# Streaming encoder trunk on one core: the first up quad's weight sums moved from VectorE to adding DMAs, two token differences moved from GpSimd to VectorE

## The reference, cut to what matters

```python
n = rms_norm(x, ln1_w); proj = n @ w_in            # 1024 x 3584, split into q k v g, gate_b gate_c hc
x = x + concatenate([retention(q,k,v,g), gate_b * conv3(gate_c * hc)]) @ w_out      # 1024 x 1024
h2 = rms_norm(x, ln2_w)
x = x + square(relu(h2 @ w_up)) @ w_down           # 1024 x 4096 and 4096 x 1024
```

## Time and profile before

| | us |
|---|---|
| median of 3 runs | 1407.86 (1407.82 to 1409.0) |
| the profiled execution's own time | 1408.8 |
| its span | 1407.1 |
| PE busy | 1377.2 (98% of the span) |
| DVE busy | 947.0 (67%) |
| ACT busy | 618.1 (44%) |
| POOL busy | 191.4 (14%) |

### The profile page before, as it was taken

The page is one execution under the profiler, slowest core; times in us unless marked ns, Lnnn a source line. Parts: engine busy times, 40 slices in busy tenths (PEclk is TensorE's granted clock), DMA queues, the critical chain, the costliest instruction groups (busy, mean ns, idle before and its releaser), DMA issues.

```text
span 1407.1 us, 21462 instructions
## 1 busy us (share of the span) xinstructions
PE 1377.2 (98%) x7702; PEld 1236.7 (88%) x7702; DVE 947.0 (67%) x1144; ACT 618.1 (44%) x736; POOL 191.4 (14%) x193
## 2 busy tenths in 40 slices
PE   8999999998999999999999999999899999999997
PEld 6888999888889899899878889998798998998986
DVE  5336415988975966867861473278889678688586
ACT  5311221466636446446543012134574464464463
POOL 2343200021000000000032430000400000000001
PEclk9999999999999999999999999999999999999999
DMA  7424203525454645555142242054166455544623
GB/s 273 135 76 121 83 1 128 134 84 122 110 159 121 145 100 142 146 118 158 31 138 96 90 121 68 3 158 140 46 150 150 103 142 145 120 120 120 150 60 105
DMA packets 93728, 162.39 MB, mean 115 GB/s; under 512 B 3956, under 2 KB 21492, under 8 KB 93624
## 3 DMA queue, kind: packets, MB, share of 16 engines
q1 hardware_dynamic: 74472, 123.18, 26.0%
q0 software_dynamic: 19008, 37.75, 15.8%
q10 hardware_dynamic: 144, 0.07, 0.0%
HBM read 153.58 MB, written 7.41 MB: 114 GB/s over the span
## 4 chain that ended last, share of the span: by engine, by line
PE 94%; DVE 2%; issue 2%; ACT 1%; POOL 1%; DMA 0%; DVEq 0%; SPq 0%; POOLq 0%; ACTq 0%
PE pair L808 27%; PE pair L867 25%; PE pair L653 15%; PE pair L663 12%; PE pair L880 8%; PE pair L703 2%; PE pair L741 1%; PE pair L748 1%; PE pair L722 1%; DVE ring L1755 1%; DVE x L1801 1%; PE pair L726 1%; PE pair L731 1%; DMA w_raw<-in_w_in 0%; PE pair L734 0%
## 5 line engine op out<-in xcount | busy, mean ns | idle before, releaser
L808 PE MATMUL pair<-mlp_in_hi,ring 128*128 128x320 f32 x1792 | 400.1, 311 | 9.8 <-DVE hidden L1780 9.8
L1141 ACT ACTIVATE ring<-raws 128x1024 fp32r<-128x1024 f32 x248 | 259.8, 1057 | 290.1 <-PE pair L867 150.2
L867 PE MATMUL pair<-ring,a_ring 128*128 128x512 f32 x1632 | 380.4, 390 | 0.0
L1755 DVE TENSOR_TENSOR ring<-raws,ring 128x1024 fp32r<-128x1024 f32 x248 | 305.2, 1241 | 101.6 <-ACT ring L1141 100.1
L867 PEld LDWEIGHTS pair<-ring,a_ring 128*128 128x128 f32 x1632 | 305.5, 188 | 63.6
L808 PEld LDWEIGHTS pair<-mlp_in_hi,ring 128*128 128x128 f32 x1792 | 302.7, 189 | 11.2 <-DVE ring L1755 10.3
L808 PE MATMUL pair<-mlp_in_lo,ring 128*128 128x320 f32 x896 | 278.2, 310 | 0.0
L808 PEld LDWEIGHTS pair<-mlp_in_lo,ring 128*128 128x128 f32 x896 | 169.6, 189 | 0.2
L663 PE MATMUL pair<-norm_hi,ring 128*128 128x320 f32 x512 | 114.5, 310 | 0.0
L1801 DVE TENSOR_TENSOR x<-x,pair 128x512 f32<-128x512 f32 x160 | 103.3, 678 | 11.4 <-PE pair L867 11.4
L653 PE MATMUL pair<-ring,norm_hi 128*128 128x512 f32 x320 | 101.6, 399 | 3.2 <-DVE norm_lo L1563 3.1
(11 more groups left out here) (153 smaller groups left out, 1686.2 us busy)
## 6 DMA issues: line engine op xcount, KB each, us to landing
raws<-in_w_mlp_up SPq DMA_DIRECT2D x32, 1024.0 KB, 5.3
raws<-in_w_mlp_down SPq DMA_DIRECT2D x32, 1024.0 KB, 5.0
w_raw<-in_w_in SPq DMA_DIRECT2D x27, 1024.0 KB, 6.1
raws<-in_w_mlp_up POOLq DMA_DIRECT2D x16, 1024.0 KB, 9.1
raws<-in_w_mlp_down POOLq DMA_DIRECT2D x16, 1024.0 KB, 8.8
raws<-in_w_out SPq DMA_DIRECT2D x8, 1024.0 KB, 8.4
past_state<-in_state_ret SPq DMA_DIRECT2D x8, 512.0 KB, 4.5
out_ret_s<-past_state SPq DMA_DIRECT2D x8, 512.0 KB, 4.9
```

The source lines that it names most:

```text
L808: mm = pe.matmul(out[:, n, 0:HALF], item_half(item, h, a)[:, k, n * P:(n + 1) * P], mlp_in[i][c][:, k], start=(i in (B11, B21, SUM_1112, B ...
L867: mm = pe.matmul(out[:], a_item[:, a, 2 * h + k, pair * P:(pair + 1) * P], item_half(item, h, c)[:, k], start=(i in (B11, B21, SUM_1112) a ...
L1141: nc.scalar.activation(item_half(item, h, 0), raw_half(quad, RAW_OF[i], h), ACT.Copy).then_inc(half_hi.sem, 1)
L1755: nc.vector.tensor_tensor(item_half(item, h, 1), raw_half(quad, RAW_OF[i], h), f(item_half(item, h, 0)), ALU.subtract).then_inc(half_lo.se ...
```

## The change

For quad 1 (the first up quad) alone, in each layer, the sums of SUM_1112 and SUM_111222 are made by DMAs of POOL's queue that add half quarters (0.5 MB) from HBM onto the slot of "11", instead of by four VectorE instructions. They signal `first_summed[h]`. The add of "22" onto "12" of quad 1 now waits only for the quarter "12" to be there, since no instruction reads the raw "12" for a sum any more. s2 and s3 are made by VectorE instead of GpSimd. The order on ACT and DVE in `up(0)` is written anew.

```diff
+BY_DMA = 1
...
 def sums_to(quad, product, half):
-    return quad * len(SUMS) + SUMS.index((product, half)) + 1
+    assert quad != BY_DMA
+    skipped = len(SUMS) if quad > BY_DMA else 0
+    return quad * len(SUMS) + SUMS.index((product, half)) + 1 - skipped
...
-        weights_summed = Signal("weights_summed", QUADS * len(SUMS))
+        weights_summed = Signal("weights_summed", (QUADS - 1) * len(SUMS))
+        first_summed = [Signal(f"first_summed{h}", 32) for h in range(2)]
...
@@ ACT, weight_half
+                    elif quad == BY_DMA:
+                        act.wait_ge(first_summed[h].sem, first_summed[h].at(layer, 16 if i == SUM_1112 else 32))
@@ ACT, up(0)
                         weight_half(item + 1, 1)
+                        weight_half(item + 2, 0)
                         read_tile(4)
                         in_diff_hi_of(0)
-                        weight_half(item + 2, 0)
+                        weight_half(item + 2, 1)
                         copy_product(b, B11, 1)
+                        weight_half(item + 3, 0)
                         in_diff_hi_of(1)
-                        weight_half(item + 2, 1)
-                        weight_half(item + 3, 0)
+                        copy_product(b, SUM_1112, 0)
+                        weight_half(item + 3, 1)
+                        copy_product(b, SUM_1112, 1)
                         in_diff_hi_of(2)
-                        copy_product(b, SUM_1112, 0)
-                        copy_product(b, SUM_1112, 1)
-                        weight_half(item + 3, 1)
                         weight_half(item + 4, 0)
+                        weight_half(item + 4, 1)
                         copy_product(b, SUM_111222, 0)
-                        weight_half(item + 4, 1)
@@ POOL
+                def add_half(i, h):
+                    quad, (last, name) = BY_DMA, {SUM_1112: (B11, "12"), SUM_111222: (SUM_1112, "22")}[i]
+                    pool.wait_ge(half_lo.sem, half_lo.at(layer, 2 * (quad * PRODUCTS + last) + h + 1))
+                    settle(pool)
+                    pool.dma_start(raw_half(quad, "11", h), quad_weights(layer, quad, name)[:, :, h * 256:(h + 1) * 256],
+                                   accum_op=ALU.add).then_inc(first_summed[h].sem, 16)
                 for quad in range(QUADS):
-                    pool.wait_ge(weights_summed.sem, weights_summed.at(layer, sums_to(quad, SUM_1112, 1)))
+                    if quad == BY_DMA:
+                        slot = slot_of(quad, "12")
+                        pool.wait_ge(slot_in[slot].sem, slot_in[slot].at(layer, 16 * (quad + 1)))
+                    else:
+                        pool.wait_ge(weights_summed.sem, weights_summed.at(layer, sums_to(quad, SUM_1112, 1)))
                     add_onto(quad, "12", "22", onto_12)
+                    if quad == BY_DMA:
+                        for h in range(2):
+                            add_half(SUM_111222, h)
                     pool.wait_ge(half_lo.sem, half_lo.at(layer, 2 * (quad * PRODUCTS + SUM_111222) + 2))
                     add_onto(quad, "11", "21", onto_11)
                     if quad == 0:
-                        for t in range(NT):
+                        for t in range(3):
                             row_rstd(layer, NT, t)
-                        last = TURN["n2", NT - 1, 1]
-                        pool.wait_ge(turn_lo.sem, turn_lo.at(layer, split_turns_to(last)))
-                        nc.gpsimd.tensor_tensor(s2_raw[:], t_diff[:], t11[:], ALU.subtract).then_inc(s2_ready.sem, 1)
-                        nc.gpsimd.tensor_tensor(t21[:], t11[:], t21[:], ALU.subtract).then_inc(s3_ready.sem, 1)
+                        add_half(SUM_1112, 0)
+                        for t in range(3, NT):
+                            row_rstd(layer, NT, t)
+                        add_half(SUM_1112, 1)
@@ DVE, up(0); next_difference makes s2, third_difference waits for s2 and makes s3
                         weight_half(item, 1)
                         normalise(layer, NT, 3, ORDER[3], 32)
+                        weight_half(item + 1, 0)
                         normalise(layer, NT, 4, ORDER[4], 32)
-                        weight_half(item + 1, 0)
                         read_turn_lo(layer, ("n2", 3, 1))
                         weight_half(item + 1, 1)
                         read_turn_lo(layer, ("n2", 4, 1))
-                        weight_sum(q, SUM_1112, 0)
+                        weight_half(item + 2, 0)
                         in_diff_lo_of(0)
-                        weight_half(item + 2, 0)
                         hidden_sum(b, B21, 0)
-                        weight_sum(q, SUM_1112, 1)
+                        weight_half(item + 2, 1)
                         hidden_sum(b, B21, 1)
-                        weight_half(item + 2, 1)
-                        weight_sum(q, SUM_111222, 0)
+                        next_difference()
+                        weight_half(item + 3, 0)
                         in_diff_lo_of(1)
-                        weight_half(item + 3, 0)
-                        weight_sum(q, SUM_111222, 1)
+                        third_difference()
                         weight_half(item + 3, 1)
                         in_diff_lo_of(2)
+                        weight_half(item + 4, 0)
+                        weight_half(item + 4, 1)
+                        last_difference()
```

More of the change, by code:

```diff
@@ L1838, in a_difference, with next_difference, third_difference @@
                     ins.then_inc(a_diff.sem, 1)
+                def next_difference():
+                    nc.vector.tensor_tensor(s2_raw[:], t_diff[:], t11[:], ALU.subtract).then_inc(s2_ready.sem, 1)
+                def third_difference():
+                    dve.wait_ge(s2_ready.sem, s2_ready.at(layer, 1))
+                    nc.vector.tensor_tensor(t21[:], t11[:], t21[:], ALU.subtract).then_inc(s3_ready.sem, 1)
                 def last_difference():
-                    dve.wait_ge(s2_ready.sem, s2_ready.at(layer, 1))
                     dve.wait_ge(s3_ready.sem, s3_ready.at(layer, 1))
```

## The result

The changed kernel is **slower**: 1420.53 us median (1416.9 to 1422.36, 6 runs) against 1408.82 us of the kernel before on the same chips, ratio 1.0075 with a 95% interval of [1.0056, 1.0095]. The forecast was 1410.1 us, and its range ended at 1416. The profiled execution took 1419.97 us, its span is 1418.3 against 1407.1. PE is busy 1376.8 us (1377.2 before), DVE 933.6 (947.0), ACT 617.0 (618.1), POOL 187.5 (191.4): no engine has more to do, and the span is 11.2 us longer by idle time of PE.

A forecast was written before the change was run, and what follows sets the result against it. PE was taken as the bound, stopped by POOL and DVE delaying each other. Ending the old stop but adding a 6.0 us one gave +1.6 and +0.6 us, in all +2.2 us: 1410.1 us, range 1401.5 to 1416.

The forecast's parts named there:

- the old stop: PE's 4.91 us wait before SUM_1112 in each layer's first up stage; forecast to vanish.
- B: DMA add for SUM_1112, half 1: issued at 307.6, landing near 314.8, with 2.5 us to spare.
- a new stop: PE before SUM_111222: forecast to stop 6.0 us, in place of 4.91 us one item earlier.
- D: DMA add for SUM_111222, half 0: issued at 313.9, 3.1 us of the engines, landing at 326.2.
- C: 1 MB DMA add of "22" onto "12": issued at 309 right behind B, 6.2 us of the engines.
- The hand-over from D's landing to PE: ACT's hi parts, then DVE's lo part, between D landed and PE beginning SUM_111222: 3.9 us.
- The low clock: PE's slower clock after the stop: 2.48 us lost, bounds 1.56 and 3.4.
- the line before D: Queue up to D's end: B 3.1, SP's loads 4.4, C 6.2, D 3.1; 16.0 us on the clock.
- Half-length packets cost as much as whole ones: Rival on B and D: 6.2 us more engine time, +14 us in all, 1421.9 us; chance 0.12.
- D taking turns with C: Rival in the add queue: D does not wait for all of C, lands at 324.2, 1404.2 us; chance 0.20.
- POOL kept from writing descriptors by VectorE: Rival at B's issue: 1.0 us later, as all behind it, +2.0 us, 1412.1 us; chance 0.06.
- E: DMA add for SUM_111222, half 1: issued about 318, landing 3 us after D, 2 us before due.

## Why the prediction was wrong

**Right.** The bound (POOL and DVE in each other's way), the old stop's end, PE running from B21 into SUM_1112, B21's start 0.2 us earlier (the last turn comes 3.93 us behind tile 3's, 4.17 before), POOL's rstd step held up by VectorE (1.41 us where it took 0.54), B's small wait, that a new stop comes ahead of SUM_111222, released by DVE's L1881 behind ScalarE's wait for D, and that C ahead of D is a cause of it (with room in the ring 6.55 of the 11.45 us are left, and 1.95 with C behind as well). The hand-over from D's landing to PE was put at 3.9 us; 330.8 to 334.80 is 4.0. The low clock was put at 2.48 us; it cost 2.54 and 2.30.

**The step that failed** is "C ("22" onto "12", 1 MB) right behind B, as it now waits for nothing new: 309. D (SUM_111222, half 0) when the low part of SUM_1112's half 0 is made: 313.9." The waits in the code were read as all that holds an issue up. C came at 314.09 and D at 324.52, because POOL had no room for their descriptors. That puts the start of each add, some 2.2 us from issue to first packet, into the line, and makes D begin when C has landed rather than when C's last packet is read. D landed at 330.7; the forecast's 326.2 is 325.3 in this execution's time. Of the difference, 5.4 us in the first layer, the larger ring took away 4.9 of PE's stop (11.45 to 6.55 us). The forecast of +2.2 us stands against a measured +2.0 us with the larger ring and +11.7 us (1420.53 - 1408.82) without. That the first two agree so closely is partly luck: with the larger ring the stops were 6.55 us in each layer for 6.0, and the low clock cost 1.8 and 2.3 us for twice 2.48. The rows of before could not show the size of the ring, since no two adds came close; but the 2048 stood in the code, and no bound was given for an issue that has to wait. It should have been a rival: adds one at a time, priced with the earlier trace rows as B + C + D from issue to landing. With 9.1 us for C and an estimated 6.0 for a half (3.1 less), D would land at 328.7 and PE stop for some 8.5 us; that B and C then took 7.8 and 10.1 us beside SP's loads makes most of the rest.

**A term mis-sized.** A half add was put at 3.1 us of the engines, half of a whole one. DMA, 327 to 332 us of the changed kernel, with all but 41 of D's 528 packets:

```profile
q0 software_dynamic: 487, 0.48, 65.7%
```

And the view of L1489, all eight half adds:

```profile
DMA to landing us min/median/max: 6.1/6.3/8.0
```

65.7% of 5 us for 487 packets makes 3.6 us for 528: half a microsecond more than by bytes, twice in the line before D, far from the 6.2 of the rival "Half-length packets cost as much as whole ones". That rival ended near the measured time (1421.9), but by a cause that is not there.

**The rivals.** D taking turns with C is out: with room in the ring D still landed 3.2 us behind all of C (326.2 and 323.0). POOL kept from writing descriptors by VectorE: B's issue took 1.34 us beside VectorE's normalisation (306.08, 1.28 us), D's and E's 1.31 and 1.29 us beside an idle VectorE, so no.

## What to carry to other kernels

A DMA issue is an instruction that can wait for room as well as for its semaphores: before more POOL DMAs are put close together, look up the ring that the kernel reserves for them and count their descriptors, and, if two do not fit, price them from issue to landing, one behind the other. In a queue that is served in order put what is due first in front, whatever is ready first. And when a change has two parts, run each alone: here one was worth 12 us (in the new order), and the other took it all back and as much again, though half of that other part, SUM_1112's sums alone, gained 2 us more.

## What the runs showed of the hardware

- An adding DMA that finds too little room in the ring shows as "issue" idle time on POOL, with no releaser; here 6.74, 9.14 and 5.20 us before C, D and E. The same label stands before the next quad's add (23.58 us), which waits for a semaphore: the landing just before the issue tells them apart.
- A ring of 2048 bytes held one add of 512 packets and took no second, three of 256 and took no fourth until the first two had landed; one of 4096 bytes held three of 512 (issued: D at 313.37, E at 317.45 and C at 318.20, with D landed only at 321.5).
- Adds of 1 KB packets cost 58% of those of 2 KB (3.6 against 6.2 us of the engines for the 528 packets of one add).
- Two GpSimd passes of 128x1280 held VectorE up for 2.5 and 2.7 us in both kernels that had them beside it (3.98 and 3.89 us in each, whichever VectorE instruction with two SBUF operands stood there, a weight half or a weight sum), and a GpSimd step of one column was held up 0.9 us by VectorE (1.41 us for 0.54).
